# Moving the first modulation pairs of a two-layer hybrid trunk inside the first projection's chunks

## The chip, the cores and the metric

One core of one Trainium2 chip runs the whole program. The metric is device time in microseconds (us) of one execution, as the median of the runs; lower is better. The engines are named as the profile names them: PE is TensorE (PEld its weight load), DVE is VectorE, ACT is ScalarE, POOL is GpSimd, and SP is the engine that issues most DMAs.

## The reference, cut to what matters

Two layers act on x (512 tokens, 1,024 channels), with a conditioning vector c:

```python
mod = silu(c) @ ada_w + ada_b
shift, scale, gate = split(mod, 3)
h = rms_norm(x, norm_g) * (1.0 + scale) + shift
proj = h @ w_in                      # cut up among three mixers
ya, yb, yc = hgrn2(...), sparse_attention(..., iq, ik, iw), s5(...)   # each times a silu gate
merged = sum over branches of sigmoid(merge_g) * (y @ w_branch)
x = x + gate * (merged @ w_out)
```

The part that matters here is the beginning of each layer: the row norm of x, the modulation rows (a vector times a 1,024 by 3,072 matrix), h out of both, and the first projection "iq", the queries of the attention's indexer (512 columns).

## The kernel before

**Tiling.** Channels lie on partitions: x is held as `xm`, eight tiles k of 128 channels by 512 tokens, and so is h. Every projection is done in float32 precision by three matmuls for each pair of tiles: h and the weights are each split into a high part (rounded by ACT) and a low part (the rest): `h_hi`, `h_lo`, `w_hi`, `w_lo`. Weights come in chunks of 512 KB. SP loads a chunk into one of four `raw` slots, ACT makes `w_hi` (line 766, three slots), then DVE (line 1264, the first four chunks only) or POOL (lines 732 and 733) makes `w_lo`. ACT may write the `w_hi` of chunk m only when PE is done with chunk m-3.

**Order.** One list, `STEPS`, written out by hand in `schedule()`, is walked by every engine from its first to its last step, and each engine issues what its own block has for the step. An engine works off its instructions strictly in this order, and engines wait for each other by semaphores. `split_upto(step)` says up to which chunk ACT and POOL make the weight parts ahead of a step; it returns 0 for the first steps, and `("low", b)` is the step that asks for chunk b at the beginning, on ACT (`w_hi`) and then on DVE (`w_lo`).

**The beginning, layer 0.** Eight steps `("xT", k)` transpose x from token rows into channel tiles on PE (line 1718), and a copy out of the bank makes `xm[k]`: on DVE for k up to 3 (line 1254), on ACT for the others (line 784). ACT sums the squares of x (line 775) and makes the inverse norm of each token. `("hs", 0)` spreads it over the partitions: DVE makes four diagonal matrices `r_diag` in `prod` (line 1258), PE multiplies ones by them (line 1750), ACT copies the result to `rb` (line 796). The modulation comes in four pairs b, each for the channel tiles 2b and 2b+1:

- `("ad0", b)`: PE makes the rows of shift and scale, 16 matmuls recorded as 32 (line 1693).
- `("low", b)`: ACT and DVE split weight chunk b.
- `("adc", b)`: ACT copies the rows to `row` (line 793); PE turns them into columns (line 1702).
- `("md0", b)`: DVE adds biases and gains (lines 1274 to 1277).
- `("hk", 0, b)`: DVE makes the two tiles `ht` (line 1322), ACT the two `h_hi` (line 822), DVE the two `h_lo` (line 1326).

The iq projection has four chunks, `("tm", 0, "iq", c)`, chunk c with channel tiles 2c and 2c+1: four token tiles t, each with two k, each with three matmuls (lines 1681 to 1683), 24 in all. It needs h of its two tiles and the split of weight chunk c. In the order before, pair b+1 stands ahead of chunk b:

```python
steps += [("ad0", 1), ("low", 1), ("adc", 1), ("md0", 1), ("hk", 0, 1)] + tm("iq", 0)
steps += [("ad0", 2), ("low", 2), ("adc", 2), ("md0", 2), ("hk", 0, 2)] + tm("iq", 1)
```

At the step `("ad0", 2)` ACT also makes the sines of the rotary tables (lines 953 and 954), which needs another activation table.

**The start of layer 1.** `("hs", 1, quarter)` are four steps: ACT squares two tiles of x each (line 805), PE sums them over the partitions (line 1757), and after the fourth ACT takes the logarithm and the exponential (lines 808 and 810). PE then does five matmuls of no use (line 1764). The tiles of h follow, and the iq chunks of layer 1, whose weights POOL finishes.

Of the kernel before, what the change touches and what calls it, by code (L numbers as in the profile page):

```python
# [26 lines left out]
ND = D // P  # L27
# [13 lines left out]
KC, NCOL = 4, 256  # L41
CHUNK = KC * NCOL
RAW_SLOTS, SPLIT_SLOTS = 4, 3
# [18 lines left out]

def schedule():

    steps = [("xT", k) for k in range(4)] + [("ad0", 0), ("hs", 0), ("low", 0), ("adc", 0)]
    for l in range(DEPTH):

        todo = [("ada", l, c) for c in range(16, 24)]
# [70 lines left out]
            return [(n[:-1], l, int(n[-1])) if n[-1].isdigit() else (n, l) for n in names]  # L139

        if l == 0:
            steps += [("md0", 0), ("hk", 0, 0)] + [("xT", k) for k in range(4, ND)]
            steps += [("ad0", 1), ("low", 1), ("adc", 1), ("md0", 1), ("hk", 0, 1)] + tm("iq", 0)
            steps += [("ad0", 2), ("low", 2), ("adc", 2), ("md0", 2), ("hk", 0, 2)] + tm("iq", 1)
            steps += [("ad0", 3), ("low", 3), ("adc", 3), ("md0", 3)] + tm("iq", 2)
            steps += [("hk", 0, 3), ("lb", 0), ("s5l", 0, 0)] + tm("iq", 3)
        else:
            steps += [("hk", l, b) for b in range(4)] + tm("iq", 0) + tm("iq", 1) + tm("iq", 2) + [("s5l", l, 0)] + tm("iq", 3)
# [74 lines left out]


STEPS = schedule()


# [34 lines left out]
DONE = done_after()  # L262
# [95 lines left out]
def split_upto(step):  # L358

    if step[0] == "xT" or step == ("hs", 0):  # L360
        return int(step[1] >= 4)
    if step[0] == "low":
        return step[1] + 1
    if DONE[step] <= 4 and step[0] in ("ad0", "adc", "md0", "hk"):
        return 0
    if step[:3] == ("tm", 0, "iq") and step[3] < 3:
        return 0
    near = FIRST[step] + len(chunks_of(step)) + RAW_SLOTS
    return min(DONE[step] + (3 if step[0] in ("gelu", "s5", "s5t") else 2), near, len(CHUNKS))
# [7 lines left out]
def program(nc, wfull, wada, x, cvec, pos, lblog, vecs, gains, s5v, s5m, consts, masks, out):  # L377
# [4 lines left out]
    with ExitStack() as ctx:  # L382
# [70 lines left out]
        hk = region(HG0 + 4096, HEADS, S)  # L453
# [12 lines left out]
        row = region(3584, S)  # L466
# [26 lines left out]
        ad_in = [region(8192 + CHUNK * i, CHUNK).rearrange("p (k w) -> p k w", k=KC) for i in range(15)]  # L493
# [22 lines left out]
        cs_sig, cs_ready = sem("cs_sig"), sem("cs_ready")  # L516
# [32 lines left out]
        def wait_free(e, key):  # L549

            b, u = BANKS.uses[key]
            if u:
                e.wait_ge(bank_read[b], u)
            return bank[b]

        def wait_full(e, key):

            b, _ = BANKS.uses[key]
            where, value = BANKS.full[key]
            e.wait_ge({"chunk": chunk_done, "ada": ada_mm}.get(where) or bank_full[where], value)  # L560
            return bank[b]

        def wait_read(e, key):

            b, u = BANKS.uses[key]
            e.wait_ge(bank_read[b], u + 1)

        def full(key):
            return bank_full[BANKS.uses[key][0]]
# [149 lines left out]
        @block.gpsimd  # L719
        def _(pool):  # L720
            lo_no = [FIRST_LOW]

            def low_parts(upto):
                while lo_no[0] < min(len(CHUNKS), upto):
                    m = lo_no[0]
                    n = m
                    pool.wait_ge(hi_done, m + 1)
                    if m == FIRST_LOW:
                        pool.wait_ge(lo_done, FIRST_LOW)
                    hi, lo = chunk_view(n, w_hi[:, m % SPLIT_SLOTS]), chunk_view(n, w_lo[:, m % SPLIT_SLOTS])  # L730
                    half = CHUNK_K[n] // 2
                    nc.gpsimd.tensor_tensor(lo[:, :half], raw_chunk(n)[:, :half], hi[:, :half].bitcast(F32), ALU.subtract)  # L732
                    nc.gpsimd.tensor_tensor(lo[:, half:], raw_chunk(n)[:, half:], hi[:, half:].bitcast(F32),  # L733
                                            ALU.subtract).then_inc(lo_done, 1)
                    lo_no[0] += 1

            for step in STEPS:
                kind, l = step[0], step[1]
                low_parts(split_upto(step))


        @block.scalar
        def _(act):
            steps = [0]
# [34 lines left out]
            for step in STEPS:  # L779
# [5 lines left out]
                if kind == "lb":  # L785
                    act.wait_ge(lb_exp, 1)
                    nc.scalar.activation(lbt[:, 2:2 + DEPTH], lbt[:, 2:2 + DEPTH], ACT.Exp).then_inc(lb_pow, 1)
                if kind == "adc":
                    b = step[1]
                    src = wait_full(act, (("ad0", b), 0))  # L790
                    if b:
                        wait_full(act, (("adc", b - 1), 0))
                    nc.scalar.activation(row, src[:], ACT.Copy).then_inc(read((("ad0", b), 0)), 1)
                if step == ("hs", 0):
                    src = wait_full(act, step)
                    nc.scalar.activation(rb, src[:], ACT.Copy).then_inc(read(step), 1)
                elif kind == "hs":
                    quarter = step[2]
                    if quarter == 3:
                        nc.scalar.activation(stat[:, 70:71], eps, ACT.Ln)  # L800
                    for k in (2 * quarter, 2 * quarter + 1):
                        wait_x(act, l, k)
                        if k >= 2:
                            act.wait_ge(sq_used, k - 1)
                        nc.scalar.activation(sq[:, k % 2], xm[:, k], ACT.Square).then_inc(sq_ready, 1)
                    if quarter == 3:
                        src = wait_full(act, ("hs", l))
                        nc.scalar.activation(rb, src[:], ACT.Ln, scale=1.0 / D, bias=eps).then_inc(read(("hs", l)), 1)
                        wait_read(act, ("hs", l))
                        nc.scalar.activation(rb, rb, ACT.Exp, scale=-0.5).then_inc(r_ready, 1)  # L810
# [865 lines left out]
        def _(pe):  # L1676
# [12 lines left out]
            def weight_rows(dst, at, halves):  # L1689

                for k in range(ND):
                    low = STRIP * (k % KC)
                    ins = mm(dst[low:low + STRIP, at:at + NCOL], cs[:, 2, k:k + 1].broadcast_to([P, STRIP]),
                             halves[k // KC][:, k % KC], start=k < KC, stop=k >= KC)
                return ins

            def to_columns(dst, from_, n):

                for i in range(n):
                    for low in (0, COL_HALF):  # L1700
                        at = i * P + low
                        ins = mm(dst[low:low + COL_HALF, i:i + 1], from_[:, at:at + COL_HALF], each_strip,
                                 start=True, stop=True)
                return ins

            pe.wait_ge(const_in, 16 * 3)
            for _ in range(WARM):
                mm(bank[4][:], ident, cst[:, 0:S], start=True, stop=True)
            for step in STEPS:
                kind, l = step[0], step[1]  # L1710
                if kind == "xT":
# [5 lines left out]
                    for t in range(NT):  # L1717
                        last = nc.tensor.transpose(dst[:, t * P:(t + 1) * P], x_tm[:, t, k * P:(k + 1) * P], ident)
                    last.then_inc(full((step, 0)), 1)
                if kind == "ad0":  # L1720
                    b = step[1]
                    dst = wait_free(pe, (step, 0))
                    pe.wait_ge(cs_ready, 1)
                    pe.wait_ge(shift_in[b], 32)
                    weight_rows(dst, 0, ad_in[4 * b:4 * b + 2])
                    pe.wait_ge(scale_in[b], 32)
                    weight_rows(dst, NCOL, ad_in[4 * b + 2:4 * b + 4]).then_inc(full((step, 0)), 1)
                if kind == "adc":
                    dst = wait_free(pe, (step, 0))
                    wait_read(pe, (("ad0", step[1]), 0))  # L1730
                    to_columns(dst, row, 4).then_inc(full((step, 0)), 1)
                if kind == "adm":

                    i = 2 * step[2] + 1
# [30 lines left out]
                if kind == "tm":  # L1765
                    key = step[:3]
                    n = FIRST[step]
                    wh, wl = split_chunk(n)
                    k0, width = CHUNKS[n][2], CHUNK_W[n]
                    for t in range(NT):  # L1770
                        dst = wait_free(pe, (key, t)) if k0 == 0 else bank[t]
                        ts = slice(t * P, (t + 1) * P)
                        for kk in range(CHUNK_K[n]):
                            k = k0 + kk
                            if t == 0:
                                pe.wait_ge(h_ready, ND * l + k + 1)
                            last = three(dst[:, 0:width], h_hi[:, k, ts], h_lo[:, k, ts], wh[:, kk], wl[:, kk],
                                         k == 0, k == ND - 1)
                        if last_chunk(step) and t < NT - 1:
                            last.then_inc(full((key, t)), 1)  # L1780
                    last.then_inc(chunk_done, 1)
                if kind == "cm":
                    _, _, name, j, kh = step
# [284 lines left out]
```

## Time and profile before

| What | Value |
|---|---|
| Median of 3 runs | 1185.37 us (1183.3 to 1186.43) |
| The profiled execution: its own time | 1183.32 us |
| Its span in the profile | 1181.5 us |
| PE busy | 1155.3 us, 98% |
| DVE, ACT, POOL busy | 861.1 us (73%), 521.7 us (44%), 493.3 us (42%) |
| Instructions | 19675 |

The span runs from the first to the last instruction that the profiler recorded; the execution's own time is 1.8 us longer. Starts are in us from the start of the span. A matmul's modelled duration overlaps the next one's start, so the pace of PE is read from starts: 0.227 us from one full matmul of iq to the next.

### The profile page before, as it was taken

How to read it: one execution, taken by the hardware profiler on the slowest of the kernel's cores; microseconds unless marked ns; L12 is line 12 of the kernel's file. 1: busy time of each engine (PE TensorE's matmuls, PEld its weight loads, DVE VectorE, ACT ScalarE, POOL GpSimd, SP SyncE). 2: the span in 40 equal slices, each digit the busy share in tenths (PEclk: the TensorE clock that was granted, in tenths of full speed). 3: DMA queues.
4: the chain of work that ended last, by engine and by line, in shares of the span. 5: the costliest groups of instructions: out<-in, count | busy, mean ns of one | idle time of the engine just before them, and what ended most of it. 6: DMA issues, size and time to landing. Idle time of an engine off the chain costs nothing.

```text
span 1181.5 us, 19675 instructions
## 1 busy us (share of the span) xinstructions
PE 1155.3 (98%) x7828; PEld 916.4 (78%) x7828; DVE 861.1 (73%) x1419; ACT 521.7 (44%) x864; POOL 493.3 (42%) x336
## 2 busy tenths in 40 slices
PE   6999999999999999999999999999999999999998
PEld 4797787887788778888768777878777878788887
DVE  4697898957488687888847589988746887777242
ACT  5554326754444344433244642456453444444321
POOL 0143451343364443545416344323425645445451
PEclk9999999999999999999999999999999999999999
DMA  9632221141323535762715222212313433455322
GB/s 353 244 128 72 74 73 55 54 141 56 107 66 83 133 96 167 272 242 107 250 36 179 90 65 75 79 54 72 115 64 98 108 91 109 118 214 217 104 72 72
DMA packets 63451, 141.88 MB, mean 120 GB/s; under 512 B 29440, under 2 KB 31744, under 8 KB 62592
## 3 DMA queue, kind: packets, MB, share of 16 engines
q1 hardware_dynamic: 54016, 137.48, 35.0%
q10 hardware_dynamic: 9344, 3.15, 1.1%
q8 instruction: 62, 1.02, 0.3%
q14 instruction: 29, 0.24, 0.1%
HBM read 127.76 MB, written 10.49 MB: 117 GB/s over the span
## 4 chain that ended last, share of the span: by engine, by line
PE 86%; DVE 8%; issue 2%; ACT 2%; DMA 1%; SPq 1%; POOL 0%; DVEq 0%; ACTq 0%
PE bank L1681 24%; PE bank L1683 24%; PE bank L1682 24%; PE bank L1824 2%; PE bank L1834 1%; PE bank L1848 1%; PE bank L1876 1%; DVE arena L1471 1%; DMA arena<-in_wada 1%; PE bank L1841 1%; PE bank L1947 1%; DVE stat L1413 1%; PE bank L1920 1%; DVE arena L1416 1%; DVE arena L1177 1%
## 5 line engine op out<-in xcount | busy, mean ns | idle before, releaser
L732 POOL TENSOR_TENSOR w_lo<-raw,w_hi 128x512 fp32r<-128x512 f32 (+1 forms) x166 | 245.4, 1478 | 667.5 <-ACT w_hi L766 667.4
L1681 PE MATMUL bank<-h_hi,w_hi 128*128 128x512 f32 x896 | 362.9, 405 | 0.0
L1683 PE MATMUL bank<-h_hi,w_lo 128*128 128x512 f32 x896 | 349.4, 390 | 0.0
L1682 PE MATMUL bank<-h_lo,w_hi 128*128 128x512 f32 x896 | 349.2, 390 | 0.0
L766 ACT ACTIVATE w_hi<-raw 128x1024 fp32r<-128x1024 f32 (+2 forms) x170 | 178.4, 1052 | 242.7 <-PE bank L1683 157.4
L733 POOL TENSOR_TENSOR w_lo<-raw,w_hi 128x512 fp32r<-128x512 f32 (+2 forms) x166 | 255.5, 1539 | 0.0
L1681 PEld LDWEIGHTS bank<-h_hi,w_hi 128*128 128x128 f32 x896 | 168.2, 188 | 42.9 <-issue 8.7
L1682 PEld LDWEIGHTS bank<-h_lo,w_hi 128*128 128x128 f32 x896 | 168.4, 188 | 38.1 <-issue 4.8
L1683 PEld LDWEIGHTS bank<-h_hi,w_lo 128*128 128x128 f32 x896 | 168.2, 188 | 35.7
L1681 PE MATMUL bank<-w_hi,h_hi 128*128 128x512 f32 (+1 forms) x256 | 97.2, 380 | 1.9 <-POOL w_lo L733 0.9
L1682 PE MATMUL bank<-w_lo,h_hi 128*128 128x512 f32 (+1 forms) x256 | 94.9, 371 | 0.0
L1683 PE MATMUL bank<-w_hi,h_lo 128*128 128x512 f32 (+1 forms) x256 | 94.7, 370 | 0.0
L1681 PE MATMUL bank<-y_hi,w_hi 128*128 128x512 f32 x224 | 91.1, 407 | 0.0
L1683 PE MATMUL bank<-y_hi,w_lo 128*128 128x512 f32 x224 | 87.4, 390 | 0.0
L1682 PE MATMUL bank<-y_lo,w_hi 128*128 128x512 f32 x224 | 87.3, 390 | 0.0
L1681 PEld LDWEIGHTS bank<-w_hi,h_hi 128*128 128x128 f32 x256 | 48.0, 188 | 12.2 <-issue 3.2
L1683 PEld LDWEIGHTS bank<-w_hi,h_lo 128*128 128x128 f32 x256 | 48.1, 188 | 7.9
L1682 PEld LDWEIGHTS bank<-w_lo,h_hi 128*128 128x128 f32 x256 | 48.1, 188 | 6.9
L1416 DVE MATCH_REPLACE8 arena<-stat,arena 128x384 f32<-128x384 f32 (+2 forms) x96 | 51.7, 544 | 0.0
L1413 DVE MAX8 stat<-arena 128x8 f32<-128x384 f32 (+2 forms) x96 | 50.3, 552 | 0.5
L1681 PEld LDWEIGHTS bank<-y_hi,w_hi 128*128 128x128 f32 x224 | 42.0, 188 | 10.0 <-issue 1.4
L1682 PEld LDWEIGHTS bank<-y_lo,w_hi 128*128 128x128 f32 x224 | 42.1, 188 | 9.7 <-issue 1.4
(285 smaller groups left out, 1660.8 us busy)
## 6 DMA issues: line engine op xcount, KB each, us to landing
raw<-in_wfull SPq DMA_DIRECT2D x170, 512.0 KB, 4.0
arena<-in_wada SPq DMA_DIRECT2D x48, 512.0 KB, 4.8
x_scratch<-xm SPq DMA_DIRECT2D x2, 2048.0 KB, 9.4
arena<-x_scratch SPq DMA_DIRECT2D x2, 2048.0 KB, 10.3
arena<-in_x SPq DMA_DIRECT2D x4, 512.0 KB, 6.3
arena<-in_s5m SPq DMA_DIRECT2D x2, 1024.0 KB, 6.2
u_scratch<-arena ACTq DMA_DIRECT2D x4, 512.0 KB, 4.7
arena<-u_scratch SPq DMA_DIRECT2D x8, 256.0 KB, 3.3
```

Of the source, the lines that this page charges most:

```text
L732: nc.gpsimd.tensor_tensor(lo[:, :half], raw_chunk(n)[:, :half], hi[:, :half].bitcast(F32), ALU.subtract)
L733: nc.gpsimd.tensor_tensor(lo[:, half:], raw_chunk(n)[:, half:], hi[:, half:].bitcast(F32), ALU.subtract).then_inc(lo_done, 1)
L766: nc.scalar.activation(chunk_view(n, w_hi[:, m % SPLIT_SLOTS]), raw_chunk(n), ACT.Copy).then_inc(hi_done, 1)
L1177: mark(v.tensor_tensor(out_, re, x_, ALU.mult))
L1413: found.append(mark(v.max(top, wk if r else acc)))
L1416: replaced[b] = mark(v.match_replace(wk, top, wk if r else acc, TAKEN))
L1471: return v.tensor_tensor(qk, qk, ends.broadcast_to([P, 2, S // m, m]), ALU.mult)
L1681: mm(out_, a_hi, b_hi, start=first, stop=False)
L1682: mm(out_, a_hi, b_lo, start=False, stop=False)
L1683: return mm(out_, a_lo, b_hi, start=False, stop=last)
L1824: mm(dst[:, 0:(b + 1) * P], iq_t[ps, h // 2, b * P:(b + 1) * P], ik_t[ps, 0:(b + 1) * P], start=True, stop=True).then_inc(full((step, 0)), 1)
L1834: mm(dst[:, 0:keys], q_t[:, h, b * P:keys], k_t[:, 0:keys], start=True, stop=True).then_inc(full((key, h)), 1)
```

## The change

It has four parts.

1. The first list of steps now has six transposes, then `("ad0", 0)`, `("low", 0)`, `("hs", 0)`, `("adc", 0)`, and only then the transposes 6 and 7. Before, four transposes, `("ad0", 0)`, `("hs", 0)`, `("low", 0)` and `("adc", 0)` stood there, and transposes 4 to 7 came after the first pair's h.
2. PE issues the rows and columns of pairs 1 to 3 inside iq chunks 0 to 2, the rows after token tile 0 and the columns after token tile 1. The other engines keep the order of steps.
3. ACT copies the rows to `row` at the step `("ad0", b)` and no longer at `("adc", b)`, that is ahead of `("low", b)` and not behind it.
4. In layer 1 ACT makes the high part of one more weight chunk between the last two squares and the logarithm, and POOL its low part.

```diff
-    steps = [("xT", k) for k in range(4)] + [("ad0", 0), ("hs", 0), ("low", 0), ("adc", 0)]
+    steps = [("xT", k) for k in range(6)] + [("ad0", 0), ("low", 0), ("hs", 0), ("adc", 0), ("xT", 6), ("xT", 7)]
...
-            steps += [("md0", 0), ("hk", 0, 0)] + [("xT", k) for k in range(4, ND)]
+            steps += [("md0", 0), ("hk", 0, 0)]
...
     if step[0] == "xT" or step == ("hs", 0):
-        return int(step[1] >= 4)
+        return int(step[1] >= 6)
...
                 low_parts(split_upto(step))
+                if kind == "hs" and step[2:] == (3,):
+                    low_parts(DONE[step] + SPLIT_SLOTS)
...
-                if kind == "adc":
+                if kind == "ad0":
                     b = step[1]
                     src = wait_full(act, (("ad0", b), 0))
...
                     if quarter == 3:
+                        high_parts(DONE[step] + SPLIT_SLOTS)
                         src = wait_full(act, ("hs", l))
...
+            def modulation_rows(b):
+
+                key = (("ad0", b), 0)
+                dst = wait_free(pe, key)
+                pe.wait_ge(cs_ready, 1)
+                pe.wait_ge(shift_in[b], 32)
+                weight_rows(dst, 0, ad_in[4 * b:4 * b + 2])
+                pe.wait_ge(scale_in[b], 32)
+                weight_rows(dst, NCOL, ad_in[4 * b + 2:4 * b + 4]).then_inc(full(key), 1)
+
+            def modulation_columns(b):
+
+                key = (("adc", b), 0)
+                dst = wait_free(pe, key)
+                wait_read(pe, (("ad0", b), 0))
+                to_columns(dst, row, 4).then_inc(full(key), 1)
+
...
-                if kind == "ad0":
-                    b = step[1]
...
+                if step == ("ad0", 0):
+                    modulation_rows(0)
+                if step == ("adc", 0):
+                    modulation_columns(0)
...
                         if last_chunk(step) and t < NT - 1:
                             last.then_inc(full((key, t)), 1)
+                        if key == ("tm", 0, "iq") and step[3] < 3 and t == 0:
+                            modulation_rows(step[3] + 1)
+                        if key == ("tm", 0, "iq") and step[3] < 3 and t == 1:
+                            modulation_columns(step[3] + 1)
```

## Rows read from the trace of the kernel before

**Rows 1.** The page, chain of work that ended last, shares by engine.
```profile
PE 86%; DVE 8%; issue 2%; ACT 2%; DMA 1%; SPq 1%; POOL 0%; DVEq 0%; ACTq 0%
```
**Rows 2.** Timeline of PE, 0 to 60 us: start, duration, line, idle before.
```profile
16.77 1.07 PE L1693 MATMUL bank<-arena,cs 128*32 128x256 f32 x16 [1.41 <-DMA arena<-in_wada]
17.77 1.16 PE L1750 MATMUL bank<-prod,cst 128*128 128x128 f32 x8
...
21.05 0.63 PE L1702 MATMUL bank<-cst,arena 128*64 128x1 f32 x16 [2.12 <-ACT arena L793]
21.61 3.48 PE L1718 MATMUL bank<-cst,arena 128*128 128x128 f32 x16
...
28.53 0.50 PE L1681 MATMUL bank<-w_hi,h_hi 128*128 128x512 f32 x1
...
34.22 1.93 PE L1693 MATMUL bank<-arena,cs 128*32 128x256 f32 x32
...
37.52 0.50 PE L1681 MATMUL bank<-w_hi,h_hi 128*128 128x512 f32 x1
...
52.06 0.39 PE L1681 MATMUL bank<-w_hi,h_hi 128*128 128x512 f32 x1
```
**Rows 3.** Timeline of ACT, the same stretch.
```profile
18.97 0.60 ACT L796 ACTIVATE arena<-bank 128x512 f32<-128x512 f32 x1 [4.76 <-PE bank L1750]
19.46 1.05 ACT L766 ACTIVATE w_hi<-raw 128x1024 fp32r<-128x1024 f32 x1
...
24.35 2.04 ACT L784 ACTIVATE xm<-bank 128x512 f32<-128x512 f32 x4
...
31.30 1.28 ACT L953 ACT_TABLE_LOAD   x1
...
33.31 1.04 ACT L766 ACTIVATE w_hi<-raw 128x1024 fp32r<-128x1024 f32 x1
36.22 0.60 ACT L793 ACTIVATE arena<-bank 128x512 f32<-128x512 f32 x1 [1.86 <-PE bank L1693]
```
**Rows 4.** Timeline of DVE, the same stretch.
```profile
14.39 0.86 DVE L1258 TENSOR_SCALAR prod<-cst,stat 128x128 f32<-128x128 f32 x4
...
20.54 1.23 DVE L1264 TENSOR_TENSOR w_lo<-raw,w_hi 128x1024 fp32r<-128x1024 f32 x1 [5.29 <-ACT w_hi L766]
21.80 0.16 DVE L1274 TENSOR_TENSOR mod<-bank,vec 128x2 f32<-128x2 f32 x1
...
37.63 0.16 DVE L1274 TENSOR_TENSOR mod<-bank,vec 128x2 f32<-128x2 f32 x1 [2.02 <-PE bank L1702]
...
38.09 1.42 DVE L1322 SCALAR_TENSOR_TENSOR arena<-xm,mod,arena 128x512 f32<-128x512 f32 x2
...
39.69 1.42 DVE L1326 SCALAR_TENSOR_TENSOR h_lo<-arena,mod,h_hi 128x512 fp32r<-128x512 f32 x2 [0.19 <-ACT h_hi L822]
```
**Rows 5.** DMAs issued from 7.9 to 8.4 us: the first weight chunk, us to landing.
```profile
raw<-in_wfull SPq DMA_DIRECT2D x1, 512.0 KB, 10.1
```
**Rows 6.** Windows: PE, PEld, DVE, ACT, POOL busy, granted clock, DMA share, GB/s.
```profile
18.98:21.00 2.02, 0.00 (x0) 0.00 (x0) 0.46 (x1) 2.02 (x3) 0.00 (x0) 1.00 1.02 408
...
22.50:23.50 1.00, 1.00 (x7) 1.00 (x6) 1.00 (x2) 0.39 (x1) 0.00 (x0) 0.50 1.03 410
```
**Rows 7.** Timeline, 55 to 90 us: DVE's last rotation of ik, PE's first transpose.
```profile
76.77 1.52 DVE L1087 TENSOR_TENSOR arena<-arena 128x256 f32<-128x256 f32 x1
...
82.72 0.60 PE L1815 MATMUL bank<-cst,arena 128*128 128x128 f32 x4
```
**Rows 8.** Timeline at the start of layer 1: ACT, then PE.
```profile
607.12 0.69 ACT L808 ACTIVATE arena<-bank,cst 128x512 f32<-128x512 f32 x1 [1.22 <-PE bank L1757]
...
620.68 1.99 ACT L766 ACTIVATE w_hi<-raw 128x1024 fp32r<-128x1024 f32 x2
...
623.06 0.39 PE L1683 MATMUL bank<-w_hi,h_lo 128*128 128x512 f32 x1
624.38 0.50 PE L1681 MATMUL bank<-w_hi,h_hi 128*128 128x512 f32 x1 [0.93 <-POOL w_lo L733]
```

More of the change, by code:

```diff
@@ L1719, in _ @@
                     last.then_inc(full((step, 0)), 1)
-                if kind == "ad0":
-                    b = step[1]
[L1722 to L1731, printed above, removed]
+                if step == ("ad0", 0):
+                    modulation_rows(0)
+                if step == ("adc", 0):
+                    modulation_columns(0)
                 if kind == "adm":
```

## The prediction, as it was made

> **What bounds the kernel now.** I read the page first. The chain of work that ended last runs through PE for 86% of the span [rows 1], so time is won or lost where PE waits, and anywhere else only if it makes PE wait. I then read the timelines of PE, ACT and DVE from 0 to 60 us, since three of the four parts of the change lie there, and the same at the start of layer 1 for the fourth. On PE the reader is to see this [rows 2]: the rows of pair 0 end at 17.84 (16.77 and 1.07), `hs` at 18.93, PE stands idle until the columns at 21.05, transposes 4 to 7 run from 21.61, and iq chunk 0 starts at 28.53. The break between chunk 0 and chunk 1, from 34.22 to 37.52, is 3.30 us long: 1.93 of rows, 0.63 of columns, and the rest a wait for ACT's copy. Chunk 3 starts at 52.06. From 37.52 to there lie two chunks and one such break, so a chunk takes (14.54 - 3.30) / 2 = 5.6 us. At 0.227 us from start to start its 24 matmuls need 5.45, and the first ones after a pause are slower. I compare the two kernels at the start of chunk 3, because from there on PE finds its work ready in both orders.
>
> ACT and DVE are half idle here, but they are serial: what an engine is told to do stands in line behind whatever its own earlier step waits for. So each wait has to be followed through their order, and not through the busy shares.
>
> **Part 1, the begin.** Rows of pair 0 end at 17.84 in both, since the landing of `ada_w` sets them [rows 2]. ACT now copies `row` first: 0.07 behind the rows (36.15 to 36.22 for pair 2 [rows 2, 3]), at 17.91. `w_hi` of chunk 0 follows 0.49 later, as it follows the copy of `rb` now [rows 3], at 18.40; the raw chunk, issued about 7.95, has landed 10.1 us later, so by about 18.05 [rows 5]. `w_lo` starts 1.08 behind `w_hi` (19.46 to 20.54 [rows 3, 4]), at 19.48, and what follows on DVE 1.26 later (20.54 to 21.80 [rows 4]), at 20.74. In the new order that is not `md0` but the four diagonal matrices (0.86 for four), which stood ready at 15.25 before [rows 4]: `low` now stands ahead of `hs` in the list. PE's `hs` starts at about 21.0 and takes 1.16 [rows 2]: 22.2. The columns end 0.63 later, at 22.8 instead of 21.68. So the first pair's `mod` comes about 1.1 us later than before.
>
> Then PE makes transposes 6 and 7. Transposes 4 to 7 took 3.48 us, 0.87 each [rows 2], at a granted clock of 0.50, the lower of the two levels (1.2 of 2.4 GHz), which came after PE had stood idle for 2 us with the clock still at 1.00 [rows 6]. The new order leaves PE idle from 17.84 to 21.0, 3.2 us, so I take the lower level again: `hs` and the columns end up to 0.4 late, at 23.2, and transpose 7 at 24.9. ACT must copy `xm[7]` (0.51, a quarter of 2.04 [rows 3]) before the first `h_hi`, because those steps now stand ahead of `hk`: copy at 25.0, `h_hi` at 25.5. `h_lo` starts about 0.8 later (1.60 from the first `ht` to the first `h_lo`, less one `ht` of 0.71 [rows 4]) and takes 0.71. Chunk 0 starts at 27.1. It was 28.53, so 1.4 us are won. At full clock it would be 26.1. Four of the transpose copies move into idle time of ACT, and cost nothing.
>
> **Parts 2 and 3, the pairs inside the chunks.** PE now does six matmuls of token tile 0 (1.5 with the slow start), then the rows (0.1 and 1.93): the rows of pair 1 end at 27.1 + 3.5 = 30.6. The question is when h for chunk 1 is ready. The chain from the end of the rows, by durations from the trace: `row` copy starts after 0.07; `w_hi` 0.49 later, since `low` now comes behind the copy on ACT; `w_lo` 1.08 later; `md0` 1.26 later, since `low` stands ahead of `md0` on DVE; the first `h_lo` starts 2.06 later (37.63 to 39.69 [rows 4]) and takes 0.71; and 0.1 to reach PE. That is 5.8 us. PE has for this time 18 matmuls and the columns: 18 x 0.227 + 0.63 + about 0.2 = 4.9 us. So it stands idle for 0.9 us at the start of each of chunks 1 to 3. Before, `w_hi` and `w_lo` were made while PE did the rows (`w_hi` at 33.31, ahead of rows at 34.22 [rows 2, 3]), and cost nothing; now that cover is gone, and they lie between rows and `md0`. This is the price of copying `row` first.
>
> From the end of one pair's rows to the end of the next: 5.8 + 1.5 + 0.1 + 1.93 = 9.3 us. Pair 2 has more: at the step `("ad0", 2)` ACT loads the sine table and makes both sines, 31.30 to 33.31, 2.0 us [rows 3]. Before, this lay ahead of any wait and was hidden under chunk 0. Now it is queued behind the `row` copy of pair 2 and ahead of `w_hi` of chunk 2, so the whole 2.0 is on the path: 11.3 us. Pair 3 then needs 5.8 us to the start of chunk 3. In sum 30.6 + 9.3 + 11.3 + 5.8 = 57.0 us, against 52.06: **5.0 us slower**. Bounds: 26.1 instead of 27.1 for the start gives 4.0.
>
> What is late next? DVE's last `h_lo` ends after chunk 3 has begun, where before it was 2 us ahead, so DVE's later work moves about 2.5 us further than PE's. DVE works without pause up to the rotation of ik, which ends at 78.3, and PE takes its first transpose from that at 82.7 [rows 7]. The 4.4 us of slack hold the 2.5; if they did not, each us over would cost one.
>
> **The clock.** PE's idle time before chunk 2 grows to 0.9 + 2.0 = 2.9 us. At 2 us idle the granted clock fell in the begin [rows 6]; the 0.7 or so inside the breaks of before did nothing. If it falls here, it does so for a stretch like that one, in which four transposes needed 3.48 us for about 1.75 us of work at full clock. So the cost is between 0 and 1.7 us, and as it does not have to fall, I take 0.7.
> The Trainium skill (TensorE: Matmul & The Clock Gate, section HAM oscillation) describes the same, matmul bursts that each start at the half clock because a wait lies between them. By that rule all 1.7 would be paid once for the gap before chunk 2, and the sum be 1.0 higher; the trace agrees in so far as the one idle stretch of 2 us is followed by 0.50.
>
> **Part 4, the start of layer 1.** Before, PE waits at the third iq chunk of layer 1 for POOL: 623.06 to 624.38 is 1.32 from start to start where 0.227 is normal [rows 8]. Its `w_hi` is the first of the two at 620.68, behind all the `h_hi`. The change makes it before the logarithm. ACT is idle for 1.22 us before the logarithm at 607.12, waiting for PE [rows 8], and a `w_hi` takes 1.05 [rows 3], so it just fits, and its slot is free, since the last chunk of `w_out` is done. Nothing is delayed by more than 0.1, POOL has no other work, and the wait of 1.1 goes, with 0.1 for the slower first matmuls: **1.2 us faster**. If it comes late for ACT's gap, up to 1.05 of it is lost again.
>
> **Sum.** 5.0 - 1.2 + 0.7 = 4.5 us slower. On the profiled execution's 1183.32 us that is 1187.8; this execution lies 2.05 below the median of the runs, so the forecast is 1189.9 us. A change under 0.3% (3.6 us) is about what this kernel's measurement can't tell from none; 4.5 is 0.38%.
>
> **Rivals.**
> - *The pairs are hidden (ends on the other side).* If the chain behind the rows were shorter than PE's 4.9 us instead of 5.8, each chunk with its pair would take 5.6 + 1.93 + 0.63 + 0.2 = 8.4 us, and chunk 3 start at 26.1 + 25.2 = 51.3, 0.8 before the old time. With part 4 that is 2.0 us faster, 1183.4 us. It needs `w_hi` and `w_lo` to leave the chain; the busy shares of ACT and DVE speak for it, the order of the steps against. 12 in 100.
> - *The clock falls more than once.* After the stalls of 0.9 us too, with the rows (1.93) at half pace in the chain: 1.9 for the next pair's rows and 1.7 for the gap make about 7 us slower in all, 1192.4 us. Idle times under 1 us in the breaks now speak against it. 12 in 100.
> - *Part 4 gives nothing*, because the logarithm moves by what POOL's wait saves: 5.7 slower, 1191.1 us. The fit of 1.05 into 1.22 is the doubt. 8 in 100.
> - *The chain as worked out*, 68 in 100, 1187.5 to 1192 us, by the start (1.0 less) and the clock (0.7 less, 1.0 more) and some noise of the median.
>
> **How the numbers follow.** The predicted time is the chain's. The range has to reach the case of hidden pairs below and the clock above: 1183.0 to 1192.5. Over 0.3% slower is above 1188.9: about 45 of the chain's 68, and nearly all of the two slower rivals, 62 in all. Faster by over 0.3% is below 1181.8, which no case gives in its centre: 5. The rest is 33.
>
> **What the changed profile would show.** Diagonals on DVE at about 20.7, behind `w_lo`; chunk 0 at about 27; `w_hi` about 0.5 behind each `row` copy, and `md0` behind `w_lo`, not behind the columns; PE waiting for `h_lo` at the start of chunks 1 to 3, most at chunk 2, with the sine table between `row` and `w_hi`; chunk 3 at about 57; PE's first transpose of layer 0's attention not waiting for DVE; no wait for POOL in layer 1. I am wrong if chunks 1 to 3 start without a wait for `h_lo`, or if the transposes of iq wait for the rotations.

## The result

| | Median | Ratio to before, 95% interval |
|---|---|---|
| before | 1184.69 us (4 runs) | |
| changed | 1194.06 us (1193.59 to 1195.35, 4 runs) | 1.0077, 1.0064 to 1.0090 |

The changed kernel is slower by 0.77%, 9.1 us at before's median; forecast were 4.5 us. The forecast time was 1189.9 us in a range from 1183.0 to 1192.5, so the time lies above the range. (Before's median was 1185.37 us from three runs then, and is 1184.69 with a fourth.) The profiled executions took 1183.32 and 1193.90 us, 10.6 us apart. The direction and the mechanism of the waits were right, the size was not.

PE in the changed kernel, in order of time (start, duration, line, idle before) follows. Line numbers move by 3 for the matmuls of the chunks (1684 to 1686 for 1681 to 1683) and for the rows (1696 for 1693); the norm is 1762 now, the transposes 1738, the columns 1705.

```profile
17.38 1.07 PE L1696 MATMUL bank<-arena,cs 128*32 128x256 f32 x16 [1.40 <-DMA arena<-in_wada]
21.57 2.08 PE L1762 MATMUL bank<-prod,cst 128*128 128x128 f32 x8 [3.12 <-DVE prod L1261]
23.57 1.02 PE L1705 MATMUL bank<-cst,arena 128*64 128x1 f32 x16
24.52 1.97 PE L1738 MATMUL bank<-cst,arena 128*128 128x128 f32 x8
28.66 0.77 PE L1684 MATMUL bank<-w_hi,h_hi 128*128 128x512 f32 x1 [2.17 <-DVE h_lo L1329]
...
31.49 3.21 PE L1696 MATMUL bank<-arena,cs 128*32 128x256 f32 x32
...
42.00 1.93 PE L1696 MATMUL bank<-arena,cs 128*32 128x256 f32 x32
...
51.80 0.77 PE L1684 MATMUL bank<-w_hi,h_hi 128*128 128x512 f32 x1 [2.77 <-DVE h_lo L1329]
...
54.63 1.93 PE L1696 MATMUL bank<-arena,cs 128*32 128x256 f32 x32
...
62.31 0.47 PE L1684 MATMUL bank<-w_hi,h_hi 128*128 128x512 f32 x1 [0.63 <-DVE h_lo L1329]
```

These rows answer to [rows 2]. Chunk 3 starts at 62.31, where it started at 52.06: 10.25 us later, and that is nearly the whole difference. PE waits for the diagonals for 3.12 us, and for h ahead of chunk 0 (2.17), chunk 1 (0.66), chunk 2 (2.77) and chunk 3 (0.63). The rows of pair 1 took 3.21 us and those of pairs 2 and 3 took 1.93.

ACT and DVE, as [rows 3] and [rows 4] showed them:

```profile
18.51 0.60 ACT L795 ACTIVATE arena<-bank 128x512 f32<-128x512 f32 x1 [2.48 <-PE bank L1696]
19.01 1.05 ACT L768 ACTIVATE w_hi<-raw 128x1024 fp32r<-128x1024 f32 x1
...
44.00 0.60 ACT L795 ACTIVATE arena<-bank 128x512 f32<-128x512 f32 x1 [3.87 <-PE bank L1696]
44.62 1.28 ACT L956 ACT_TABLE_LOAD   x1
...
46.63 1.04 ACT L768 ACTIVATE w_hi<-raw 128x1024 fp32r<-128x1024 f32 x1
```
```profile
20.09 1.23 DVE L1267 TENSOR_TENSOR w_lo<-raw,w_hi 128x1024 fp32r<-128x1024 f32 x1 [4.77 <-ACT w_hi L768]
21.23 0.87 DVE L1261 TENSOR_SCALAR prod<-cst,stat 128x128 f32<-128x128 f32 x4
...
47.71 1.22 DVE L1267 TENSOR_TENSOR w_lo<-raw,w_hi 128x1024 fp32r<-128x1024 f32 x1 [6.74 <-ACT w_hi L768]
48.86 0.15 DVE L1277 TENSOR_TENSOR mod<-bank,vec 128x2 f32<-128x2 f32 x1
...
50.91 1.41 DVE L1329 SCALAR_TENSOR_TENSOR h_lo<-arena,mod,h_hi 128x512 fp32r<-128x512 f32 x2 [0.19 <-ACT h_hi L825]
```

The chain of pair 2 can be read from top to bottom: rows end at 43.93, copy, table of the sines, high part at 46.63, low part, `md0` at 48.86 and `h_lo` at 50.91, with no gap over 0.2 us, while the columns had long been there.

What was not foreseen is in the windows. Each line gives the length, the busy time of PE, PEld, DVE, ACT and POOL, the granted clock, and the load of the DMA engines:

```profile
21.60:22.50 0.90, 0.90 (x4) 0.90 (x5) 0.50 (x3) 0.00 (x0) 0.00 (x0) 0.50 1.04 414
...
28.50:34.20 5.70, 5.54 (x34) 3.15 (x38) 0.68 (x2) 0.00 (x0) 0.00 (x0) 0.51 1.03 410
34.20:37.50 3.30, 3.30 (x37) 2.25 (x30) 1.14 (x2) 1.54 (x2) 0.00 (x0) 1.00 1.04 397
...
50.00:54.00 4.00, 2.20 (x5) 1.82 (x6) 2.13 (x4) 1.33 (x2) 0.00 (x0) 0.65 0.39 127
```

The clock is at the lower level (1.2 GHz) from about 20.5 us on, inside the wait ahead of the norm. It is still there in the first quarter of chunk 0 (token tile 0) and in the rows of pair 1, until about 34 us, and it falls again at chunk 2, from about 51 to 54.6 us. In before's profile it was down from about 21.9 to 25.2 us, for transposes 4 to 7 [rows 6].

In layer 1 the wait of [rows 8] is gone. The added high part fits ahead of the logarithm, with 0.27 us of idle time of ACT left where there had been 1.22:

```profile
616.97 1.04 ACT L768 ACTIVATE w_hi<-raw 128x1024 fp32r<-128x1024 f32 x1
618.29 0.69 ACT L811 ACTIVATE arena<-bank,cst 128x512 f32<-128x512 f32 x1 [0.27 <-PE bank L1769]
```

### The profile page after: what moved, and what is told of

It is laid out like the page before. It is cut to its first block, busy times and chain, and to the rows that moved or that the text cites. A ratio compares the mean times of both kernels' runs of the same rounds, so it can differ in the third digit from the quotient of the medians.

```text
span 1192.1 us, 19675 instructions
## 1 busy us (share of the span) xinstructions
PE 1162.2 (97%) x7828; PEld 918.6 (77%) x7828; DVE 859.5 (72%) x1419; ACT 521.4 (44%) x864; POOL 489.3 (41%) x336
## 3 DMA queue, kind: packets, MB, share of 16 engines
q8 instruction: 62, 1.02, 0.4%
## 4 chain that ended last, share of the span: by engine, by line
PE 82%; DVE 10%; issue 3%; ACT 2%; DMA 2%; SPq 1%; POOL 0%; DVEq 0%; ACTq 0%
PE bank L1684 23%; PE bank L1686 22%; PE bank L1685 22%; PE bank L1840 2%; PE bank L1850 1%; PE bank L1864 1%; DMA arena<-in_wada 1%; PE bank L1892 1%; DVE arena L1474 1%; PE bank L1857 1%; PE bank L1963 1%; PE bank L1696 1%; ACT w_hi L768 1%; DVE stat L1416 1%; PE bank L1936 1%
## 5 line engine op out<-in xcount | busy, mean ns | idle before, releaser
L732 POOL TENSOR_TENSOR w_lo<-raw,w_hi 128x512 fp32r<-128x512 f32 (+1 forms) x166 | 242.4, 1460 | 682.2 <-ACT w_hi L768 682.0
```

## The experiments

Each kernel was timed in turn with the kernel before; the difference in us is the ratio's, at 1184 us, and its interval is about 1 us to each side, up to 1.5 for the kernels with few runs. The changed kernel is 9.1 us slower than before, and a difference against it is good to about 2 us. The last column says how far the profiled execution, from which all rows are read, lies from the median of its kernel: those of c1 and b4 lie far above, and their rows show more loss than is typical. Even a1, whose begin is that of before, starts chunk 3 1.5 us later than before's profile does.

| Kernel | Ratio, 95% interval | Against before | Chunk 3 starts | Profile less median |
|---|---|---|---|---|
| a1 weight alone | 0.9991 (0.9983 to 1.0000) | -1.1 | 53.54 | +0.5 |
| a2 begin undone | 1.0038 (1.0025 to 1.0051) | +4.5 | 56.39 | -0.9 |
| a3 row copy back | 1.0026 (1.0017 to 1.0036) | +3.1 | 57.32 | +1.1 |
| a4 PE kept busy | 1.0025 (1.0016 to 1.0035) | +3.0 | 55.68 | +0.9 |
| b1 begin and weight | 1.0007 (0.9999 to 1.0016) | +0.8 | 53.47 | -0.4 |
| b2 sines early | 1.0044 (1.0031 to 1.0057) | +5.2 | 58.67 | +0.6 |
| b3 norm first | 1.0037 (1.0024 to 1.0050) | +4.4 | 57.00 | 0.0 |
| b4 row first alone | 1.0008 (1.0000 to 1.0017) | +0.9 | 54.63 | +1.6 |
| c1 both undone | 0.9991 (0.9982 to 0.9999) | -1.1 | 52.99 | +3.3 |
| c2 both undone, kept busy | 1.0003 (0.9995 to 1.0012) | +0.4 | 53.32 | +0.7 |
| e1 pairs inside, busy early | 0.9980 (0.9971 to 0.9989) | -2.4 | 50.55 | -0.4 |
| e2 old order, busy early | 1.0004 (0.9995 to 1.0013) | +0.5 | 54.38 | 0.0 |

**a1, part 4 alone**, on the kernel before:

```diff
                 low_parts(split_upto(step))
+                if kind == "hs" and step[2:] == (3,):
+                    low_parts(DONE[step] + SPLIT_SLOTS)
...
                     if quarter == 3:
+                        high_parts(DONE[step] + SPLIT_SLOTS)
```

> The kernel before with the fourth part alone: one more weight chunk split ahead of the logarithm in layer 1. My theory: the wait of PE for POOL at the third iq chunk of layer 1 (1.1 us, 624.38 less 623.06 less 0.23) is gone, and nothing is moved, since the high part took 1.04 us in a gap of ACT and the logarithm of the changed kernel still began 0.2 us after PE's last square sum: 1.2 us faster than before. Rival: ACT's logarithm is late by the same amount, and the time is within 0.3 us of before.

Measured: 1.1 us faster, with an interval that just reaches 1. It agrees with the theory (1.2), and the rival (nothing) is at the very edge of the interval. The trace speaks for the theory: PE is 1.5 us later than before when the sums of squares of layer 1 are done (608.45 against 606.92) and 0.3 us later at the next transposes (660.95 against 660.65), so 1.2 us came back in between.

**a2, the old begin** under the changed rest:

```diff
-    steps = [("xT", k) for k in range(6)] + [("ad0", 0), ("low", 0), ("hs", 0), ("adc", 0), ("xT", 6), ("xT", 7)]
+    steps = [("xT", k) for k in range(4)] + [("ad0", 0), ("hs", 0), ("low", 0), ("adc", 0)]
...
-            steps += [("md0", 0), ("hk", 0, 0)]
+            steps += [("md0", 0), ("hk", 0, 0)] + [("xT", k) for k in range(4, ND)]
...
-        return int(step[1] >= 6)
+        return int(step[1] >= 4)
```

> The changed kernel with the old begin (four transposes, norm before the first weight chunk, transposes 4 to 7 behind the first h), all else as changed. Theory of the clock: the begin costs most, because in the changed kernel PE stood idle for 3.1 us before the norm, and chunk 0 with the rows of pair 1 then ran at half clock; with the old begin chunk 0 starts near 25 us at the full level, where the changed kernel starts it at 28.66, and the rows of pair 1 end near 28.7 where they end at 34.70: 5.5 to 7 us faster than the changed kernel. Rival, chain alone: only the later start counts, 28.66 against 27 or so, and the waits behind the rows give it back: under 2.5 us faster.

Measured: 4.6 us faster than the changed kernel, less than expected and over the rival. Chunk 0 starts at 24.98, after 3.5 us of idle PE, and at about 25.6 the clock fell here too: the rows of pair 1 ran from 27.27 for 2.77 us, not 1.93. The begin costs about half of the loss. My 5.5 to 7 us took full pace for chunk 0 and the rows; but with pair 1's rows moved inside the chunk, the old begin leaves PE idle ahead of chunk 0 as well.

**a3, the copy of the rows behind the high part again**:

```diff
-                if kind == "ad0":
+                if kind == "adc":
                     b = step[1]
                     src = wait_full(act, (("ad0", b), 0))
```

> The changed kernel with ACT's copy of the rows moved back behind the weight chunk's high part (at adc), the pairs still inside the chunks. Theory of the chain: high and low part leave the chain from the rows to h, and so do the sines; the waits of PE at chunks 1 to 3 (about 0.9, 2.8 and 0.6) fall under 0.2 us each, the time from the end of one pair's rows to the next falls from 9.2 and 12.6 us to about 8.4, and with no wait of 2.8 the granted clock stays at 1.00 from 34 us on: 6 us faster than the changed kernel (5 to 7). Rival: h of the next pair is late for another reason (DVE's products, ACT's h_hi), and at most 2 us are won.

Measured: 6.0 us faster than the changed kernel, as expected, and the rival (at most 2) is out. PE from the trace of a3:

```profile
41.58 1.93 PE L1696 MATMUL bank<-arena,cs 128*32 128x256 f32 x32
...
50.23 1.93 PE L1696 MATMUL bank<-arena,cs 128*32 128x256 f32 x32
```

From rows to rows it is 8.65 us, against 12.63 (42.00 to 54.63) in the changed kernel: no wait for h is left at chunks 1 to 3. The rows of pair 1 are still slow (3.22 us), since the begin is as in the changed kernel.

**a4, PE kept busy in three waits** by matmuls of no use, nothing else touched:

```diff
+                    for _ in range(3):
+                        mm(dst[:], ident, cst[:, 0:S], start=True, stop=True)
                     for t in range(NT):
                         pe.wait_ge(diag_ready, t + 1)
...
+                    if key == ("tm", 0, "iq") and step[3] in (0, 2):
+                        for _ in range(2 if step[3] == 0 else 3):
+                            mm(wait_free(pe, (("ad0", step[3] + 1), 0))[:], ident, cst[:, 0:S], start=True, stop=True)
                     wh, wl = split_chunk(n)
```

> The changed kernel with extra matmuls of no use on PE in three waits: three before the norm's matmuls, two before iq chunk 0 and three before chunk 2 (0.89 us each at full clock), into banks that are overwritten; no data of the kernel changes. Theory of the clock: the waits stay as long as they are, but the granted clock stays at 1.00 or comes back before chunk 0, so that chunk 0's first six matmuls take 1.5 us and not 2.8, the rows of pair 1 1.9 and not 3.2, the norm's matmuls 1.2 and not 2.1: 4 to 6 us faster than the changed kernel, though it does more work. Rival, no clock effect: these matmuls lie in waits and change nothing, or cost up to 1 us.

Measured: 6.1 us faster than the changed kernel, although PE has more work. The clock was at 1.00 from 18 to 56 us, and over all ten timed executions its mean was 0.999 to 1.000, where the four of the changed kernel had 0.991 to 0.993. PE from its trace:

```profile
17.71 2.84 PE L1761 MATMUL bank<-cst 128*128 128x512 f32 x6
...
25.86 0.47 PE L1684 MATMUL bank<-w_hi,h_hi 128*128 128x512 f32 x1 [0.51 <-DVE h_lo L1329]
27.42 1.93 PE L1696 MATMUL bank<-arena,cs 128*32 128x256 f32 x32
...
46.46 0.47 PE L1684 MATMUL bank<-w_hi,h_hi 128*128 128x512 f32 x1 [0.19 <-DVE h_lo L1329]
...
55.68 0.47 PE L1684 MATMUL bank<-w_hi,h_hi 128*128 128x512 f32 x1 [0.64 <-DVE h_lo L1329]
```

This is the decisive run. With the clock held, chunk 0 starts at 25.86 and chunk 3 at 55.68. The prediction's sum for full clock gives 26.1 and 56.0, and a kernel 2.8 us slower than before (4.0 less 1.2) where 3.0 were measured. Chunk 3 starts 6.6 us earlier than in the changed kernel; 0.7 of that is the earlier landing of the scale's weights (16.71 against 17.38), which differs between executions.

**b1, the new begin with the pairs outside** (the kernel before with the two edits of `steps`, that of `split_upto`, and part 4):

> The kernel before with the new begin (part 1) and the weight chunk of layer 1 (part 4), without the pairs inside the chunks and with the old place of the copy of the rows. Theory: the begin alone costs, by its later norm (diagonals behind the low part) and the half clock that follows PE's idle time; here the rows of pair 1 stand ahead of chunk 0 and fill the wait for h, so less of it hurts than in the changed kernel: 2 to 4 us slower than before, after 1 us won by part 4. Rival: the begin is hidden behind the rows of pair 1, and the kernel is 1 us faster than before.

Measured: 0.8 us slower than before, so 1.9 slower than a1. The theory had 2 to 4 slower, the rival 1 faster: it lies between them, and neither came out. The rows of pair 1 are slow here too (25.88 for 2.69 us), but they stand in the wait for h.

**b2, the sines early**:

```diff
-                if step == ("ad0", 2):
+                if step == ("adc", 0):
                     act.wait_ge(ang_ready, 1)
```

> The changed kernel with the sines moved from the step of pair 2's rows to that of pair 0's columns, where ACT waited 3.6 us for the norm. Theory: 2.0 us leave the chain of pair 2, PE's wait before chunk 2 falls from 2.8 to about 0.7 us, the clock doesn't fall there (1.3 us more), and DVE's rotations are waited for by less: 3.0 to 3.5 us faster than the changed kernel. Rival: only the 2.0 us of the chain (the clock falls anyway): 2 us.

Measured: 3.9 us faster than the changed kernel, a little more than expected. The rows of pair 3 start 9.24 us after those of pair 2, and not 12.63: 3.4 us for 2.0 us of work moved. a2 lies between, at 11.36: the sines are there as in the changed kernel, but the clock did not fall. So the sines are 2.1 us of it and the clock 1.3. The time alone doesn't exclude the rival (2 us), which is at the edge of what the intervals allow; the trace does, as PE's wait ahead of chunk 2 is 0.64 us and the clock stays at 1.00.

**b3, norm before the first weight chunk**:

```diff
-[("ad0", 0), ("low", 0), ("hs", 0), ("adc", 0), ("xT", 6), ("xT", 7)]
+[("ad0", 0), ("hs", 0), ("low", 0), ("adc", 0), ("xT", 6), ("xT", 7)]
```

> The changed kernel with the norm's step ahead of the first weight chunk again (hs before low), the six transposes and all else as changed. Theory: DVE's diagonals no longer stand behind the low part, PE's norm starts at about 18 us and not at 21.6, chunk 0 at about 24.8 and not at 28.7; PE is still idle for some 4 us before chunk 0, so the rows of pair 1 stay slow; the chain behind them is as in the changed kernel: 3 to 5 us faster than the changed kernel. Rival: the start of chunk 0 is set by the raw chunk and by ACT, and less than 1.5 us are won.

Measured: 4.7 us faster than the changed kernel, as expected, by one swap in a list. PE from its trace:

```profile
24.95 0.77 PE L1684 MATMUL bank<-w_hi,h_hi 128*128 128x512 f32 x1 [4.12 <-DVE h_lo L1329]
27.78 2.89 PE L1696 MATMUL bank<-arena,cs 128*32 128x256 f32 x32
...
47.77 0.47 PE L1684 MATMUL bank<-w_hi,h_hi 128*128 128x512 f32 x1 [2.77 <-DVE h_lo L1329]
49.33 1.93 PE L1696 MATMUL bank<-arena,cs 128*32 128x256 f32 x32
```

The idle time of 4.12 us ahead of chunk 0 is the longest of all, and chunk 0 starts at half pace. At chunk 2 PE is idle for the same 2.77 us as in the changed kernel, and yet it starts at full pace (0.47 and not 0.77 for its first matmul). So a wait of this length may or may not lower the clock.

**b4, part 3 alone** on the kernel before:

```diff
-                if kind == "adc":
+                if kind == "ad0":
                     b = step[1]
```

> The kernel before with the copy of the rows moved ahead of the weight chunk's high part (part 3) and nothing else. Theory: with the pairs ahead of the chunks, h of pair 1 has a whole chunk of time, so the longer chain costs nothing; the first columns and transposes 4 to 7 come earlier: within 0.3% of before, 0 to 1 us faster. Rival: the chain behind the rows costs in this order too (2 us and more slower than before).

Measured: 0.9 us slower, with an interval from 0 to 2. I had expected 0 to 1 us faster. The rival's 2 us and more are at its edge. From the trace:

```profile
22.58 1.93 PE L1693 MATMUL bank<-arena,cs 128*32 128x256 f32 x32
28.17 1.02 PE L1702 MATMUL bank<-cst,arena 128*64 128x1 f32 x16 [3.65 <-ACT arena L793]
29.11 0.79 PE L1681 MATMUL bank<-w_hi,h_hi 128*128 128x512 f32 x1
...
36.79 1.93 PE L1693 MATMUL bank<-arena,cs 128*32 128x256 f32 x32
```

The rows of pair 1 came earlier than before (22.58 against 25.02), but the columns waited for ACT, and PE stood idle for 3.65 us. Chunk 0 started 0.6 us later than before and then took 7.68 us instead of 5.69 (28.53 to 34.22 [rows 2]), with the clock at the lower level. So what was won at the rows was lost to a new wait and to the clock. This execution lies 1.6 us above its median, so the typical loss is smaller.

**c1, begin and copy undone** (the edits of a2 and a3 together):

> The changed kernel with the old begin and the copy of the rows back behind the weight's high part: what is left are the pairs inside the chunks and the weight chunk in layer 1. Theory: chunk 0 starts at 25.0 as in the kernel with the old begin, after 3.5 us of idle PE, so its end and the rows of pair 1 run at half clock (2.8 us instead of 1.9); then 8.65 us a chunk: chunk 3 starts at about 52.3 where the kernel before has 52.06. With 1.0 us from layer 1: 0.8 us faster than before (0 to 1.5). Rival, the pairs inside the chunks cost by themselves (PE's switch between the kinds of matmul): slower than before by 1 us or more.

Measured: 1.1 us faster than before, as expected. The rival, that the pairs inside cost by themselves, is out. But a1, with part 4 alone, is faster by the same 1.1, so here the pairs inside win nothing either. In the profiled execution, the slowest of twelve and 3.3 us above their median, chunk 3 started at 52.99, 0.7 later than expected.

```profile
25.02 0.77 PE L1684 MATMUL bank<-w_hi,h_hi 128*128 128x512 f32 x1 [0.68 <-ACT xm L786]
27.85 2.71 PE L1696 MATMUL bank<-arena,cs 128*32 128x256 f32 x32
```

**c2, the same with three matmuls of no use before chunk 0**:

```diff
+                    if step == ("tm", 0, "iq", 0):
+                        for _ in range(3):
+                            mm(wait_free(pe, (("ad0", 1), 0))[:], ident, cst[:, 0:S], start=True, stop=True)
                     wh, wl = split_chunk(n)
```

> The same as the kernel with both undone, with three matmuls of no use in PE's idle time before iq chunk 0 (0.9 us each, into the bank of pair 1's rows). Theory of the clock: the granted clock stays at 1.00, the rows of pair 1 take 1.93 us and end at 28.5, chunk 3 starts at about 50.7: 2.4 us faster than before, 1.5 us faster than without the extra matmuls. Rival: the extra matmuls end after h is ready, and nothing is won over the kernel with both undone.

Measured: 0.4 us slower than before, so 1.5 slower than c1: the rival and worse, nothing was won and some was lost. The rows say why:

```profile
21.55 3.48 PE L1738 MATMUL bank<-cst,arena 128*128 128x128 f32 x16
24.87 2.74 PE L1782 MATMUL bank<-cst 128*128 128x512 f32 x6
27.04 0.79 PE L1684 MATMUL bank<-w_hi,h_hi 128*128 128x512 f32 x1
```

The clock fell at about 21.3 us, just after the wait before the columns had ended; the transposes took 3.48 us, and so there was no idle time left where I had put the matmuls. They delayed chunk 0 by 2.0 us (27.04 against 25.02). The place to act is the wait ahead of the fall, which e1 tries.

**e1, c1 with two such matmuls in the wait before the first columns**:

```diff
                 dst = wait_free(pe, key)
+                for _ in range(2 if b == 0 else 0):
+                    mm(dst[:], ident, cst[:, 0:S], start=True, stop=True)
                 wait_read(pe, (("ad0", b), 0))
```

> The pairs inside the chunks and the weight chunk in layer 1, with the old begin and the old place of the copy, and with two matmuls of no use (0.9 us each) in PE's 2.1 us wait before the first columns. Theory of the clock: it stays at 1.00, transposes 4 to 7 take 2.0 us and not 2.7 to 3.5, the rows of pair 1 take 1.93 us, chunk 3 starts at about 50.7: 2.4 us faster than before (0.9980), 1.3 us faster than without these matmuls. Rival: PE's idle time only moves to before chunk 0, the clock falls there, and the time is that of the kernel with both undone (1 us faster than before).

Measured: 0.9980, 2.4 us faster than before, as expected, and the fastest of all. The 1.3 us against c1 are as expected too, but the two intervals overlap, so by time alone they are not shown. The clock is at 1.00 from 10 to 56 us:

```profile
18.36 1.88 PE L1724 MATMUL bank<-cst 128*128 128x512 f32 x4
20.65 0.63 PE L1705 MATMUL bank<-cst,arena 128*64 128x1 f32 x16 [0.40 <-ACT arena L795]
21.21 1.97 PE L1740 MATMUL bank<-cst,arena 128*128 128x128 f32 x16
24.62 0.47 PE L1684 MATMUL bank<-w_hi,h_hi 128*128 128x512 f32 x1 [1.45 <-ACT xm L786]
26.18 1.93 PE L1696 MATMUL bank<-arena,cs 128*32 128x256 f32 x32
```

**e2, the order before with part 4 and the same two matmuls**:

> The kernel before with the weight chunk in layer 1 and the same two matmuls of no use before the first columns, pairs ahead of the chunks as before. Theory: transposes 4 to 7 take 2.0 us and not 3.5, and then PE does the rows of pair 1, but the columns wait for ACT, whose copies of the transposes and high part set chunk 0 to about 28: 0 to 0.5 us over what layer 1 gives, so 1.0 to 1.5 us faster than before. Against it, the kernel with the pairs inside is 1 us faster still, if what it saves (the waits of 0.8 us before each pair's columns) is real.

Measured: 0.5 us slower than before, where 1.0 to 1.5 faster was expected. In its trace the columns of pair 1 wait 2.52 us for ACT (28.70), and chunk 0 then runs from 29.26 to 36.53, 7.3 us instead of 5.7. PE's idle time had only moved to a place where chunk 0 pays for it. Against e1, 2.9 us lie between the two orders, clear of the intervals. In the two profiles 1.6 of them is chunk 0 at half pace in e2. So with the same two matmuls the pairs inside are worth having, where in c1, without them, they won nothing.

## Why the prediction was wrong

**The term that failed is the clock: 0.7 us, with 1.7 as its bound.** I let the clock fall in the begin for the norm, the columns and the transposes only, and took full pace from chunk 0 on, in the step "six matmuls of token tile 0 (1.5 with the slow start), then the rows (0.1 and 1.93)". In the trace, from the start of chunk 0 to the end of the rows of pair 1, it took 34.70 - 28.66 = 6.0 us, not 3.5. That is 2.5 us that no term had.

The gap before chunk 2 cost another 1.3: from the end of pair 2's rows to the end of pair 3's it was 12.6, not 11.3 (a2, where the clock did not fall there, has 11.4). The bound of 1.7 took four transposes for 1.75 us of work at full clock; in a2 they took 1.97, so the row it came from stands for 1.5. The norm and columns at half pace took 2.08 and 1.02, 1.3 us more than at full pace, where I had given 0.4.

What I had in hand was the row that shows it: 2 us of idle PE, then 0.50 [rows 6]. I counted the idle time before the norm, and overlooked that the wait for h ahead of chunk 0, 2.2 us in my own numbers (24.9 to 27.1), is a second one. Such a wait is enough by itself: in a2 and b3 there is no wait ahead of the norm, PE is idle for 3.5 and 4.1 us ahead of chunk 0, and the rows of pair 1 take 2.77 and 2.89 us. How the changed kernel's 2.5 us split between its two waits (3.1 and 2.2 us, with the clock down all the way between them) no run shows.

That the clock is the term, run a4 shows: with the clock held at 1.00, 6.1 of the 9.1 us are gone.

The rest, by the steps:

- *The begin.* Diagonals behind the low part, as worked out: 21.23, 0.5 later than forecast. Chunk 0 at 28.66 instead of 27.1. Of the 1.6, 0.6 is the landing of the scale's weights, later in this execution (17.38 against 16.77), the rest the half clock. So part 1 did not win 1.4 us: chunk 0 starts 0.1 later than before, or 0.5 earlier if the landing is taken off. b3 shows the price of the swapped norm, 4.7 us with what follows from it.
- *The chain behind the rows.* Right. From rows to rows 9.2 (forecast 9.3), from the rows of pair 3 to chunk 3 5.75 (5.8). With the clock held, chunk 3 starts at 55.68 for a forecast of 56.0. a3 and b2 confirm the two members, the copy's place and the sines. The sum checks: 62.31 - 57.0 = 5.3 us, which are 1.6 + 2.5 + 1.3, less 0.1.
- *DVE's slack.* Forecast that 4.4 us would hold 2.5. The 2.5 were right (the last `h_lo` ends 12.75 us later than before, chunk 3 starts 10.25 later), but DVE's next steps took 3.2 us more than before, and the rotation of ik ended at 94.20 where it had ended at 78.29. The slack had been read a little short too: the transposes at 82.72 are those of iq, and the first that needs ik started at 83.16, so there were 4.9 us. PE waited 0.58 us:

```profile
94.26 0.66 PE L1824 MATMUL bank<-cst,arena 128*128 128x128 f32 x4 [0.58 <-DVE arena L1090]
```

- *Layer 1.* The wait went, and the logarithm was not delayed. Alone it is worth 1.1 us (a1), forecast 1.2. In the changed kernel's profile PE's lateness is 11.2 us at the sums of squares (614.46 against 603.30) and 9.9 at the next transposes (670.57 against 660.65), so 1.2 came back. At the end it is 10.6, with a wait late in layer 1 that before doesn't have (a1's profile has one of 0.40, those of c1 and e1 have none; what brings it is open):

```profile
1068.03 0.50 PE L1684 MATMUL bank<-h_hi,w_hi 128*128 128x512 f32 x1 [0.53 <-POOL w_lo L733]
```

- *The rivals.* That the clock falls more than once had 12 in 100 and a price of about 7 us; that is what happened, and it cost more. I priced it for stalls under 1 us, where it did not happen, and not for those of 2 us.

Undoing the begin alone wins 4.6, the copy's place alone 6.0, and together they win 10.2, so these two nearly add up. Keeping PE busy without undoing anything wins 6.1, and this can't be added to them: a wait removed can take the lower clock with it, as a3 and b2 did at chunk 2.

Left open: whether the clock would fall at the 2.77 us wait before chunk 2 in every execution (it did in the changed kernel's profile, and did not in those of a2 and b3), and so how its 1.3 us spread over the timed runs. The mean clock of the four executions (0.991 to 0.993, the profiled one 0.992) can't tell, as these 3.5 us at half clock move it by only 0.0015.

## What to carry to other kernels

Price a wait of PE by its length and by what stands behind it: after waits of 2 to 4 us the work behind them often ran at half pace here, so look at which work will lie there, also behind waits that a change only moves. Useless matmuls helped in the waits ahead of the fall, sized below the wait (a4, e1), won nothing where the idle time only moved on (e2), and delayed the work when they came after the fall (c2). In a list of steps that several engines walk, a step moved for one engine is moved for all: read what stands behind the first blocking wait on each.

## What the runs showed of the hardware

The granted clock took both ways with idle times of the same length: it was 1.00 through 2.75 us at chunk 2 of a2 and 2.77 of b3, and fell at 2.77 in the changed kernel and after 2.1 in the begin of before. A shorter one was no guarantee either. The begin of a1 is that of before, and PE waits for the same DMA ahead of the second half of pair 0's rows. Before, the wait was 1.41 us and these rows took 1.07 [rows 2]; in a1 they took 1.94, at a granted clock of 0.50 (b4 has the same):

```profile
16.77 1.94 PE L1696 MATMUL bank<-arena,cs 128*32 128x256 f32 x16 [1.40 <-DMA arena<-in_wada]
```

Nor did the fall always come while PE was idle. In c1 the clock was 1.00 through the wait of 2.1 us and for another 1.4 us of columns and transposes, and fell between 22.4 and 22.8 us. So one profile doesn't price a wait.

DVE's rotation steps were longer where POOL worked beside them. The same steps of ik took 0.42 us before, all but the last, which fell beside POOL's work too (1.52 [rows 7]), and in the changed kernel, where they fell beside POOL's low parts, 1.4 to 1.5:

```profile
88.80 1.40 DVE L1083 TENSOR_TENSOR arena<-arena,sin_t 128x256 f32<-128x256 f32 x1
90.12 1.51 DVE L1084 TENSOR_TENSOR arena<-arena,sin_t 128x256 f32<-128x256 f32 x1
...
92.99 0.41 DVE L1087 TENSOR_TENSOR arena<-arena,cos_t 128x256 f32<-128x256 f32 x1
```
```profile
88.18 1.74 POOL L733 TENSOR_TENSOR w_lo<-raw,w_hi 128x512 fp32r<-128x512 f32 x1
89.88 1.47 POOL L732 TENSOR_TENSOR w_lo<-raw,w_hi 128x512 fp32r<-128x512 f32 x1
91.31 1.48 POOL L733 TENSOR_TENSOR w_lo<-raw,w_hi 128x512 fp32r<-128x512 f32 x1
```

The rotation of ik took 5.4 us so, where it had taken 3.5: that is 1.9 of the 3.2 us by which DVE ran later than forecast. POOL's low parts end at 92.8, and the next rotation step is short again. The Trainium skill (GPSIMD Engine Reference, section Architecture) says that GpSimd and VectorE share one physical read port and one write port of the SBUF; the trace agrees in that both engines' instructions are longer where they overlap: POOL's took 1.27 us at 89.13 before, with DVE idle, and 1.47 to 1.74 here. No experiment here tested it by itself.
